# The mLSTM value and output-gate slabs by seven products of halves, as fillers of the attention

## The chip, the cores and the metric

The kernel runs on one core of a Trainium2 chip. The core has a matrix engine (TensorE, PE in the rows), a vector engine (VectorE, DVE), a scalar engine (ScalarE, ACT), GpSimd (POOL), and a sync engine (SP) that here only issues transfers and waits for semaphores. Each engine works through its own list in order; semaphores tie the lists together. The metric is the device time of one execution in microseconds (us). Everything is float32.

## What is computed

One layer of a decoder trunk on 256 tokens of width 2048: a norm, one input projection that feeds three mixers (a sparse attention with a compressed, a selected and a window branch; an mLSTM; a convolution), one output projection, a residual add, a second norm, and a mixture of 32 experts of which each token takes two.

```python
(q, k_c, v_c, k_s, v_s, k_w, v_w, g_nsa, mq, mk, mv, mo, mi, mf, cu) = jnp.split(h @ w_in, points, axis=-1)
a_out = nsa_attention(q, k_c, v_c, k_s, v_s, k_w, v_w, g_nsa, ...)
hm = mlstm_chunkwise(mq, mk, mv, mi + mlstm_i_bias, mf + mlstm_f_bias)
hm = jax.nn.sigmoid(mo) * hm
...
return jnp.concatenate([a_out, hm, c], axis=-1) @ w_out
...
hb = jax.nn.silu(xb @ w_gate[e]) * (xb @ w_up[e])      # for each expert e
y += (hb @ w_down[e]) * wt
```

The change concerns `mv` and `mo`: 1024 columns of `h @ w_in`, four slabs of 256 columns (`mv0`, `mv1`, `mo0`, `mo1`).

## The kernel before

**Slabs and units.** The input weights come in slabs of 2048 x 256 into a ring of six slots in SBUF (`ring`, slab n in slot n mod 6). Fifteen slabs (`FAST_SLABS`) are multiplied by seven products of halves: the 256 tokens, the 2048 inputs and the 256 columns are halved, and seven products of 128 x 1024 by 1024 x 128 (`m1` to `m7`, each 8 matmuls of 128 columns on TensorE) with sums on VectorE take the place of eight. The token sums (`tok_s1` to `tok_s4`) are made once and lie in `x1`. The weight sums are made for each slab by VectorE: `left_sums` (two instructions), `right_sum` and `last_sum` (one each), all on 128 x 1024 elements, and seven short adds put the products together (`combine`, and the copy in `keep_m1`). The last four slabs, `mv0` to `mo1`, are plain: 8 units of 16 matmuls of 256 columns, 128 in all.

**The attention.** Those 128 matmuls are fillers: `fill(n)` puts the next n of them between the steps of the attention, so that TensorE has work while VectorE and ScalarE work on the scores. The attention has four parts s = 0 to 3. `scores(s, n)` multiplies queries by keys, pair by pair (8 pairs in parts 0 and 1, 4 in parts 2 and 3), with n fillers behind each pair; each pair waits until VectorE has taken the pair before it out of the one PSUM buffer (`biased`). On VectorE `biases(s)` adds the position term to each pair and reduces for the maximum after every second pair (every pair in parts 2 and 3). ScalarE takes the exponents, VectorE scales them (`gated(s)`, which ends in `p_ready`), and `attend(s, n)` on TensorE transposes them block by block and multiplies by the values, with n fillers in each block (5 blocks in parts 0 and 1). The order on TensorE is scores 0, scores 1, attend 0, scores 2, attend 1, scores 3, `mlstm_values`, and then attend 2, attend 3 and the output projection; on VectorE it is biases 0, biases 1, gated 0, gated 1, biases 2, and so on. The scores of parts 0 and 2 lie in `spare`, those of parts 1 and 3 in `x1`, whose token sums are done with by then. ScalarE copies each finished plain unit out of PSUM (`late_saves`).

**The output projection and the experts.** The output weights come in four column parts m (`OUT_SLOTS` names the ring slots). Part 0 runs as plain matmuls (`out_part`), parts 1 to 3 by seven products of halves (`product`). SP then streams 403 MB of expert weights through the ring and other buffers; every transfer waits for the TensorE product that frees its buffer (`load_chunk`: `prod_done` in the output projection, `w_used` in the experts).

Of the kernel before, what the change touches and what calls it, by code (L numbers as in the profile page):

```python
# [19 lines left out]
ALU = mybir.AluOpType  # L20
# [3 lines left out]
P = 128  # L24
# [3 lines left out]
DK = D // P  # L28
# [10 lines left out]
RING = 6  # L39
# [149 lines left out]
UNITS = projection_units()  # L189

FAST_SLABS = ("ca0", "ca1", "mq0", "mq1", "mk0", "mk1", "vc0", "ks0", "kw0", "vs0", "q0", "q1", "q2", "q3", "vw0")
FAST = [u for u, (n, _, kind, _, i) in enumerate(UNITS) if SLABS[n] in FAST_SLABS and i == 0]
# [26 lines left out]
LATE = units_before("mv")  # L219


# [17 lines left out]
CHUNK_SLOT = [3, 4, 0, 5, 1, 2]  # L239
CHUNK_INC = 16  # L240
# [52 lines left out]
TILES_BY = [sum(2 * HPG * (t + 1) for p, t in STEPS[:s]) for s in range(len(STEPS) + 1)]  # L293
LATE_STEPS = (len(UNITS) - LATE) * DK
SLOPES = [2.0 ** (-8.0 * (h + 1) / HEADS) for h in range(HEADS)]


def build(nc, x, attn_norm_g, w_in, cmp_pos_k, cmp_w1_k, cmp_w2_k, cmp_pos_v, cmp_w1_v, cmp_w2_v, nsa_out_g,
# [3 lines left out]
    with ExitStack() as ctx:  # L302
# [10 lines left out]
        x1 = sb("x1", [P, TT, D])  # L313
# [20 lines left out]
        def mb(name, shape, dt=F32):  # L334
# [41 lines left out]
        sc = [tile.rearrange("p (g h b k) -> p g h b k", g=2, h=HPG, b=2)  # L376
              for tile in (att[:, :], x1[:, :, :].rearrange("p t d -> p (t d)"))]
        osq = hid[:, :]
# [50 lines left out]
        tok_21, tok_22 = hT[:, 0:8, P:2 * P], hT[:, 8:16, P:2 * P]  # L429
        in_t3, in_t2 = (tile[:, :, :].rearrange("p a b -> p (a b)").rearrange("p (k n) -> p k n", k=8) for tile in (mv, mo))  # L430

        def quarter(u, high, right):
# [215 lines left out]
        def _(sp):  # L648
# [268 lines left out]
        def _(pe):  # L917
# [117 lines left out]
            def mlstm_values():  # L1035
                pe.wait_ge(unit_saved, units_with("mv"))
                pe.wait_ge(biased, TILES_BY[-1])
# [124 lines left out]
            def late_step():  # L1162

                u, k = LATE + late[0] // DK, late[0] % DK
                n, part, kind, s, i = UNITS[u]
                if k == 0:
                    pe.wait_ge(w_loaded[n % RING], slab_at[n])
                    pe.wait_ge(unit_saved, LATE - 2 if u == LATE else u - 1)
                mm = pe.matmul(PS[:, unit_bank(u), 0:256], hT[:, k, i * P:(i + 1) * P], ring[:, n % RING, k, :],  # L1169
                               start=(k == 0), stop=(k == DK - 1))  # L1170
                if k == DK - 1:
                    mm.then_inc(unit_done, 1)
                late[0] += 1
# [686 lines left out]
        def _(act):  # L1860
# [132 lines left out]
            def save_unit(u):  # L1993
# [14 lines left out]
                elif kind == "folded":  # L2008
                    b = b[:, 0:128].rearrange("p (t n) -> p t n", t=TT)
                    step(act.activation(gates[:, :, 0:48], b[:, :, 0:48], ACT.Sigmoid, bias=ZERO_C))  # L2010
                    return act.activation(gates[:, :, 48:56], b[:, :, 48:56], ACT.Copy)
                elif part == "mv":
                    dst = mv[:, i, s * 256:(s + 1) * 256]
                elif part == "mo":
                    dst = mo[:, i, s * 256:(s + 1) * 256]
                elif part in ("kc", "vc"):
# [27 lines left out]

            late = [LATE]

            def late_saves(n):
                for u in range(late[0], late[0] + n):
                    act.wait_ge(unit_done, u + 1)
                    save_unit(u).then_inc(unit_saved, 1)  # L2050
                late[0] += n

            def exponents(s, saves):

                p, t = STEPS[s]
                u, w = s % 2, P * (t + 1)
                for i in range(HPG):
# [6 lines left out]
                    e.then_inc(exp_done, 1)  # L2064
                    if i == 1:
                        late_saves(saves)
                act.wait_ge(cmp_shifted, s + 1)
# [18 lines left out]

            def attend_saves(s, saves):
                for j in range(len(BLOCKS_OF[s])):
                    turned_saves(s, j)
                    if s == 3 and j == 1:  # L2090
                        pieces["mlstm_root"]()
                    if j == 3:
                        late_saves(saves)
                head_saves(s)
# [4 lines left out]

            exponents(0, 0)  # L2100
            late_saves(1)
            exponents(1, 1)
            late_saves(2)
            attend_saves(0, 1)
            exponents(2, 0)
            late_saves(1)
            attend_saves(1, 1)
            head_root(0)
            exponents(3, 0)
            late_saves(1)  # L2110
            act.wait_ge(unit_saved, len(UNITS))
            act.activation(mo[:, :, :], mo[:, :, :], ACT.Sigmoid, bias=ZERO_C).then_inc(mo_gated, 1)
            head_root(1)
            attend_saves(2, 0)
            attend_saves(3, 0)
            mlstm_result()
# [206 lines left out]
        def _(dve):  # L2323
# [364 lines left out]
            def mlstm_norm():  # L2688
# [3 lines left out]
                    .then_inc(hm_norm, 1)  # L2692

            biases(0)
# [456 lines left out]
```

## Time and profile before

| | before |
|---|---|
| median of 3 runs | 1425.89 us (1425.21 to 1428.28) |
| the profiled execution's own time | 1428.03 us |
| its span, first to last instruction | 1426.2 us |
| TensorE busy | 1205.7 us, 85% of the span |
| VectorE busy | 483.6 us, 34% |
| ScalarE busy | 255.3 us, 18% |
| HBM read | 476.05 MB, 335 GB/s over the span |
| chain that ended last | TensorE 52%, transfers 43% |

How to read it: an engine's busy time is the sum of its instructions. The span lies 1.83 us under the execution's own time. The chain that ended last is followed back from the last instruction, at each step to what released it; work off this chain can grow without cost until it gets onto it. A busy share is a mean over stages with different limits, so the rows below go by stage.

### The profile page before, as it was taken

The page shows a single profiled execution, that of the slowest core. Times are in us where ns is not written, and L with a number is a line of the kernel's source. Part 1 is how long each engine was busy: PE and PEld are TensorE (multiplying, and loading weights), DVE is VectorE, ACT ScalarE, POOL GpSimd, SP SyncE. Part 2 cuts the span into 40 slices and gives each one's busy share as a digit, 9 for nine tenths or more (in the row PEclk, how much of TensorE's full clock was granted, in tenths as well). Part 3 has the DMA queues.
Part 4 walks back from the last instruction along what each step waited for, and adds up shares of the span by engine and source line. Part 5 has one row for each costly group of instructions (what it writes and reads, how often), then busy time and mean ns, then how long its engine had stood idle before and what let it go on. Part 6 is the DMA issues. An engine that isn't in the chain of part 4 may idle for free.

```text
span 1426.2 us, 17903 instructions
## 1 busy us (share of the span) xinstructions
PE 1205.7 (85%) x7431; PEld 708.9 (50%) x7431; DVE 483.6 (34%) x1001; ACT 255.3 (18%) x629; POOL 13.5 (1%) x82
## 2 busy tenths in 40 slices
PE   8999999999999998669689958768587695876977
PEld 7999999766568753123244314224142241422422
DVE  5398997663875431121110220111101111011123
ACT  2101111444600122011111101002020010201112
POOL 2000000000010000000000000000000000000000
PEclk9999999999999999889999989989899898998989
DMA  9958677431644899999999999999999999999995
GB/s 318 274 158 194 167 161 236 119 82 38 165 112 166 346 413 426 429 427 427 428 428 428 426 428 427 427 427 429 428 426 427 429 427 425 431 426 426 429 427 237
DMA packets 133362, 479.34 MB, mean 336 GB/s; under 512 B 47804, under 2 KB 105632, under 8 KB 107552
## 3 DMA queue, kind: packets, MB, share of 16 engines
q1 hardware_dynamic: 126816, 477.58, 85.9%
q10 hardware_dynamic: 6464, 0.58, 0.4%
q8 instruction: 61, 1.00, 0.3%
q14 instruction: 21, 0.17, 0.0%
HBM read 476.05 MB, written 2.10 MB: 335 GB/s over the span
## 4 chain that ended last, share of the span: by engine, by line
PE 52%; DMA 43%; ACTq 2%; DVE 1%; ACT 1%; issue 1%; DVEq 0%
DMA ring<-in_expert_w_up_dram 36%; PE PS L1127 13%; PE PS L1447 10%; DMA spare<-in_expert_w_up_dram 6%; PE PS L1269 5%; PE PS L1169 3%; PE PS L1434 3%; PE PS L1246 2%; PE PS L1638 2%; ACTq L1862 2%; PE PS L1425 1%; PE PS L1221 1%; PE PS L1119 1%; PE PS L1648 1%; PE PS L1188 1%; PE PS L1509 1%
## 5 line engine op out<-in xcount | busy, mean ns | idle before, releaser
L1447 PE MATMUL PS<-ring,XG 128*32 128x512 f32 x1296 | 222.2, 734 | 147.9 <-DMA ring<-in_expert_w_up_dram 107.3
L1447 PEld LDWEIGHTS PS<-ring,XG 128*32 128x32 f32 x1296 | 57.6, 131 | 274.9 <-issue 271.8
L3068 DVE TENSOR_TENSOR hTe<-PS,sg 128x128 f32<-128x128 f32 (+1 forms) x31 | 9.9, 320 | 349.3 <-ACT sg L2193 349.1
L2885 DVE TENSOR_TENSOR x<-PS,x 128x1024 f32<-128x1024 f32 x41 | 50.2, 1225 | 209.8 <-PE PS L1526 208.4
L2181 ACT ACTIVATE Hs<-PS 128x512 f32<-128x512 f32 x30 | 17.9, 597 | 463.1 <-PE PS L1447 349.8
L1434 PE MATMUL PS<-ring,XG 128*64 128x512 f32 x192 | 84.6, 594 | 18.0 <-DMA ring<-in_expert_w_up_dram 14.5
L1526 PE MATMUL PS<-Y,SW 128*128 128x512 f32 (+2 forms) x176 | 90.6, 627 | 1.5 <-ACT ro L2289 1.5
L1447 PE MATMUL PS<-spare,XG 128*32 128x512 f32 x208 | 66.0, 793 | 27.8 <-DMA ring<-in_expert_w_up_dram 27.8
L1436 PE MATMUL PS<-ring,XG 128*64 128x512 f32 x192 | 85.0, 595 | 0.0
L1425 PEld LDWEIGHTS PS<-sel,xn 128*128 128x128 f32 x640 | 75.3, 191 | 13.0 <-issue 12.7
L1425 PE MATMUL PS<-sel,xn 128*128 128x128 f32 x640 | 77.6, 280 | 1.4 <-DVE x L2885 1.4
L1127 PE MATMUL PS<-hT,ring 128*128 128x128 f32 x624 | 73.4, 275 | 0.7 <-ACT mix L2031 0.7
L1127 PEld LDWEIGHTS PS<-hT,ring 128*128 128x128 f32 x624 | 71.7, 192 | 1.9 <-issue 1.7
L3079 DVE COPY Y<-PS 32x512 f32<-32x512 f32 x46 | 31.8, 692 | 118.0 <-PE PS L1509 117.6
L1509 PE MATMUL PS<-ring,hTe 128*32 128x512 f32 x608 | 70.5, 596 | 0.0
L2161 ACT ACTIVATE XG<-PS,ffn_gk 128x128 f32<-128x128 f32 (+1 forms) x176 | 54.1, 358 | 65.3 <-PE PS L1425 54.1
L1169 PE MATMUL PS<-ring,hT 128*128 128x256 f32 x256 | 64.3, 392 | 0.0
L1434 PEld LDWEIGHTS PS<-ring,XG 128*64 128x64 f32 x192 | 25.3, 137 | 71.9 <-issue 71.9
L1169 PEld LDWEIGHTS PS<-ring,hT 128*128 128x128 f32 x256 | 45.8, 189 | 19.7 <-issue 14.9
L1526 PEld LDWEIGHTS PS<-Y,SW 128*128 128x128 f32 (+2 forms) x176 | 29.4, 192 | 41.7 <-issue 39.7
L1127 PE MATMUL PS<-x,ring 128*128 128x128 f32 x416 | 48.6, 275 | 0.0
L2466 DVE SCALAR_TENSOR_TENSOR mix<-spare,taps,mix 128x256 f32<-128x256 f32 x120 | 48.4, 481 | 0.0
(494 smaller groups left out, 1577.2 us busy)
## 6 DMA issues: line engine op xcount, KB each, us to landing
ring<-in_expert_w_up_dram SPq DMA_DIRECT2D x53, 2048.0 KB, 23.8
ring<-in_expert_w_gate_dram SPq DMA_DIRECT2D x53, 2048.0 KB, 26.9
ring<-in_expert_w_down_dram SPq DMA_DIRECT2D x51, 2048.0 KB, 27.1
ring<-in_w_in_dram SPq DMA_DIRECT2D x17, 2048.0 KB, 9.5
spare<-in_expert_w_gate_dram SPq DMA_DIRECT2D x9, 2048.0 KB, 26.2
spare<-in_expert_w_up_dram SPq DMA_DIRECT2D x8, 2048.0 KB, 23.9
spare<-in_expert_w_down_dram SPq DMA_DIRECT2D x8, 2048.0 KB, 27.3
ring<-in_w_in_dram SPq DMA_DIRECT2D x16, 512.0 KB, 7.3
```

Of the source, the lines that this page charges most:

```text
L1127: mm = pe.matmul(dst, left[:, k], right[:, k], start=(k == 0), stop=(k == 7))
L1169: mm = pe.matmul(PS[:, unit_bank(u), 0:256], hT[:, k, i * P:(i + 1) * P], ring[:, n % RING, k, :], start=(k == 0), stop=(k == DK - 1))
L1269: mm = pe.matmul(PS[:, 4 + n // 2, 256 * (n % 2):256 * (n % 2) + 256], left[:, k, :], right[:, k, :], start=(k == 0), stop=(k == 7))
L1425: mm = pe.matmul(PS[:, 6 + f % 2, (k % 2) * P:(k % 2) * P + rows_of_group(q)], xn[:, t, k, :], sel[:, t, 0:rows_of_group(q)], start=(t == ...
L1434: gate = pe.matmul(PS[0:width, bank, :], x_, weight_rows(gate_slot, 4 * (c % 2) + j), start=(c == 0 and j == 0), stop=(c == 3 and j == 3))
L1436: up = pe.matmul(PS[64:64 + width, bank, :], x_, weight_rows(up_slot, 4 * (c % 2) + j), start=(c == 0 and j == 0), stop=(c == 3 and j == 3))
L1447: mm = pe.matmul(PS[r:r + 32, 0, :], gathered_rows(q, 4 * c + j)[:, column:column + 32], weight_rows(slots[u], 4 * (c % 2) + j), start=(c ...
L1509: mm = pe.matmul(PS[32 * b:32 * b + 32, 2, :], hTe[:, k, 0:32], w[:, j, 512 * b:512 * b + 512], start=(k == 0), stop=(k == 3))
L1526: mm = pe.matmul(PS[:, 4 + 2 * cols + b, :], SW[0:rows, buf, t * P:(t + 1) * P], Y2[0:rows, buf, (2 * cols + b) * 512:(2 * cols + b + 1) * ...
L2161: ins = act.activation(gathered_rows(q, k)[:, 0:rows], PS[:, 6 + f % 2, P * i:P * i + rows], ACT.Copy, scale=ffn_gk[:, k:k + 1])
L2466: ins = dve.scalar_tensor_tensor(out=cacc[:, c, :], in0=src, scalar=w, in1=cacc[:, c, :], op0=ALU.mult, op1=ALU.add)
L2885: dve.tensor_tensor(y, new, old, ALU.add).then_inc(sc_added, 1)
```

## The change

The four slabs `mv0` to `mo1` join the slabs that are multiplied by seven products of halves. The fillers are now 4 x 7 x 8 = 224 matmuls of 128 columns instead of 128 of 256 columns. VectorE makes the weight sums of each slab (`late_left_sums`, `late_right_sums`, `late_end_sum`: four instructions) and puts the products together (`late_first`, `late_last`: eight short ones), placed by hand between the parts of the attention; ScalarE's copies of the units go. The token sums stay in `x1` until the fillers are done, so that the scores of parts 1 and 3 move from `x1` to ring slot 1, and the weight sums lie in ring slot 2. The output weights and the expert chunks take the ring slots in another turn. The first two column parts of the output weights now go into slots that the last four slabs leave, and wait for those.

```diff
-OUT_SLOTS = [(1, 2), (3, 4), (0, 5), (1, 2)]
+OUT_SLOTS = [(3, 4), (5, 0), (1, 2), (3, 4)]
-TURN = [SPARE, 3, 4, 0, 5, 1, 2]
+TURN = [SPARE, 5, 0, 1, 2, 3, 4]
...
             for m, pair in enumerate(OUT_SLOTS):
-                if m < 3:
+                if m < 2:
                     sp.wait_ge(unit_done, max(last_use[s] for s in pair))
-                else:
-                    sp.wait_ge(p_turned, 2 * PAIRS_BY[-1])
+                elif m == 2:
                     for t in range(TT):
                         sp.dma_start(x1[:, t, :], x[0, t * P:(t + 1) * P, :]).then_inc(x_again, 16)
+                    sp.wait_ge(p_turned, 2 * PAIRS_BY[-1])
+                else:
                     sp.wait_ge(out_done, TT)
...
             def late_step():
+                i, r = divmod(late[0], 8 * len(LATE_PRODUCTS))
+                name, k = LATE_PRODUCTS[r // 8], r % 8
+                j, u = FAST_LATE + i, LATE_SLABS[i]
                 if k == 0:
+                    if name == "m2":
+                        pe.wait_ge(first_scaled if i else unit_saved, SCALED + 2 * i - 1 if i else LATE - 2)
+                    if name == "m5":
+                        pe.wait_ge(first_scaled if i else unit_saved, SCALED + 2 * i if i else LATE)
+                    if name in ("m6", "m4"):
+                        pe.wait_ge(w_summed, 4 * j + {"m6": 3, "m4": 4}[name])
+                mm = pe.matmul(late_part(name), tokens[:, k], weights[:, k], start=(k == 0), stop=(k == 7))
...
-            fill(8)
+            fill(16)
             pe.wait_ge(unit_saved, LATE)
             pe.wait_ge(cmp_saved, 1)
-            scores(0, 2)
+            scores(0, 5)
             scores(1, 3)
-            fill(16)
+            fill(32)
             pe.wait_ge(sT_ready, ML_H)
-            attend(0, 4)
-            scores(2, 3)
-            attend(1, 4)
+            attend(0, 7)
+            scores(2, 5)
+            fill(1)
+            attend(1, 7)
             mean_square(0)
-            scores(3, 3)
+            scores(3, 5)
             fill(LATE_STEPS)
             mlstm_values()
             pe.wait_ge(conv_out, CT)
-            pe.wait_ge(unit_saved, len(UNITS))
+            pe.wait_ge(first_scaled, LATE_SAVED)
...
+            late_left_sums(0)
+            late_right_sums(0)
+            late_end_sum(0)
+            late_left_sums(1)
             biases(0)
+            late_first(0)
+            late_last(0)
+            late_right_sums(1)
             biases(1)
+            late_end_sum(1)
             gated(0)
+            late_first(1)
+            late_left_sums(2)
+            late_last(1)
             gated(1)
+            late_right_sums(2)
+            late_end_sum(2)
+            late_first(2)
             biases(2)
+            late_last(2)
+            late_left_sums(3)
+            late_right_sums(3)
+            late_end_sum(3)
             head_squares(0)
             gated(2)
+            late_first(3)
             biases(3)
+            late_last(3)
             head_norm(0)
```

Among the fillers the products of a slab come in the order m2, m1, m6, m7, m5, m3, m4. Product m2 of a slab waits for `late_first` of the slab before it (its PSUM bank), m6 for the slab's right sum, and m4 for its end sum.

Two places show how the lists of the engines move. The first is VectorE's list behind the last slab of the input projection: the rows of before run from the last add of that slab to the first maximum of the scores of part 0. `spare` holds those scores, `w` the compressed ones.

```order
L2425 TENSOR_TENSOR PS<-PS,pT 128x128
L2618 SCALAR_TENSOR_TENSOR w<-dist_c,PS 128x16
L2620 SCALAR_TENSOR_TENSOR spare<-dist,PS 128x2x128
L2618 SCALAR_TENSOR_TENSOR w<-dist_c,PS 128x16
L2620 SCALAR_TENSOR_TENSOR spare<-dist,PS 128x2x128 x3
L2625 TENSOR_REDUCE rs<-spare 128x2x2
```

The same place in the changed list, from the same last add to the first score row; lines 2709 to 2727 are weight sums.

```order
L2434 TENSOR_TENSOR PS<-PS,pT 128x128
L2709 TENSOR_TENSOR ring<-ring 128x1024
L2712 TENSOR_TENSOR ring<-ring 128x8x128
L2719 TENSOR_TENSOR ring<-ring 128x1024
L2727 TENSOR_TENSOR ring<-ring 128x8x128
L2709 TENSOR_TENSOR ring<-ring 128x1024
L2712 TENSOR_TENSOR ring<-ring 128x8x128
L2627 SCALAR_TENSOR_TENSOR w<-dist_c,PS 128x16
```

Six instructions of 128 x 1024 elements now stand between the input projection and the first scores. The second place is VectorE's list between the scores of part 0 and those of part 1 in the changed kernel; before, the first score row of part 1 followed the row of line 2639 (2630 then) directly. `mv`, `upto` and `cmask` take the put-together products here.

```order
L2639 TENSOR_TENSOR w<-w,rs 128x128
L2735 COPY upto<-PS 128x128
L2736 TENSOR_TENSOR mv<-PS,upto 128x128
L2737 TENSOR_TENSOR upto<-PS,upto 128x128
L2738 TENSOR_TENSOR cmask<-PS,upto 128x128
L2747 TENSOR_TENSOR upto<-PS,upto 128x128
L2748 TENSOR_TENSOR mv<-PS,cmask 128x128
L2749 TENSOR_TENSOR mv<-PS,cmask 128x128
L2751 TENSOR_TENSOR mv<-PS,upto 128x128
L2719 TENSOR_TENSOR ring<-ring 128x1024
L2627 SCALAR_TENSOR_TENSOR w<-dist_c,PS 128x16
```

Nine instructions, eight short and one of 128 x 1024, moved in between two parts of the scores.

## Rows read from the trace of the kernel before

**Rows 1.** The page: its head line and the transfer engines' line of the slices.

```profile
span 1426.2 us, 17903 instructions
...
DMA  9958677431644899999999999999999999999995
```

**Rows 2.** Windows by stage: stretch, length; busy (count) PE, PEld, DVE, ACT, POOL; clock, DMA share, GB/s.

```profile
265.90:308.40 42.50, 41.58 (x194) 27.64 (x193) 29.92 (x86) 24.81 (x81) 0.00 (x0) 1.00 0.40 100
...
478.00:552.00 74.00, 71.78 (x538) 43.98 (x534) 23.22 (x95) 20.71 (x54) 0.00 (x0) 1.00 0.99 408
552.00:1426.20 874.20, 664.45 (x3842) 274.33 (x3842) 129.62 (x212) 118.37 (x278) 0.00 (x0) 0.91 0.99 420
```

**Rows 3.** The chain that ended last, in order of time: start, length, what.

```profile
412.58 37.99 PE PS L1269 x176
...
553.98 15.95 DMA ring<-in_expert_w_up_dram
```

**Rows 4.** SP's waits from 430 to 510: total, times, longest.

```profile
SPq L687 <- PE PS L1269: 62.6, 5, 25.0
```

**Rows 5.** The same chain: a fast slab, and plain fillers in one piece, in twos and threes.

```profile
252.24 12.50 PE PS L1127 x112
...
266.05 3.46 PE PS L1169 x16
...
270.17 1.06 PE PS L1169 x4
...
287.15 1.49 PE PS L1169 x6
```

**Rows 6.** VectorE's timeline, 249 to 329: start, length, line, tiles, [wait and releaser].

```profile
249.04 1.23 DVE L2383 TENSOR_TENSOR mv<-ring 128x1024 f32<-128x1024 f32 x1 [5.14 <-PE PS L1127]
250.30 1.23 DVE L2386 TENSOR_TENSOR ring<-ring 128x1024 f32<-128x1024 f32 x1
...
265.98 0.29 DVE L2425 TENSOR_TENSOR PS<-PS,pT 128x128 f32<-128x128 f32 x1
...
271.93 0.75 DVE L2620 SCALAR_TENSOR_TENSOR spare<-dist,PS 128x256 f32<-128x256 f32 x2 [0.81 <-PE PS L1188]
272.72 1.22 DVE L2625 TENSOR_REDUCE rs<-spare 128x4 f32<-128x1024 f32 x1
...
303.77 4.29 DVE L2649 TENSOR_SCALAR spare<-spare,rs 128x256 f32<-128x256 f32 x16
...
328.21 0.17 DVE L2618 SCALAR_TENSOR_TENSOR w<-dist_c,PS 128x16 f32<-128x16 f32 x1 [14.46 <-PE PS L1188]
```

**Rows 7.** TensorE's timeline, 272 to 309, same columns.

```profile
272.88 0.73 PE L1188 MATMUL PS<-keys,nsa_q 64*128 64x272 f32 x4
...
276.51 0.73 PE L1188 MATMUL PS<-keys,nsa_q 64*128 64x272 f32 x4
...
286.45 0.70 PE L1188 MATMUL PS<-keys,nsa_q 64*128 64x256 f32 x4 [0.45 <-DVE x L2620]
...
308.41 1.06 PE L1203 MATMUL PS<-ident,spare 128*128 128x128 f32 x8
```

**Rows 8.** Window of one load of output weights, columns as in Rows 2.

```profile
308.40:325.90 17.50, 17.49 (x95) 12.19 (x96) 5.21 (x21) 6.17 (x12) 0.00 (x0) 1.00 0.97 240
```

**Rows 9.** TensorE's timeline behind four waits in the expert stage.

```profile
599.74 5.34 PE L1447 MATMUL PS<-ring,XG 128*32 128x512 f32 x32 [4.73 <-DMA ring<-in_expert_w_up_dram]
...
707.43 3.64 PE L1447 MATMUL PS<-ring,XG 128*32 128x512 f32 x32 [2.09 <-DMA ring<-in_expert_w_up_dram]
...
836.28 4.08 PE L1447 MATMUL PS<-ring,XG 128*32 128x512 f32 x24 [3.39 <-DMA ring<-in_expert_w_up_dram]
...
895.05 0.61 PE L1434 MATMUL PS<-ring,XG 128*64 128x512 f32 x1 [2.72 <-DMA spare<-in_expert_w_up_dram]
```

**Rows 10.** Windows right behind the last two of these waits, columns as in Rows 2.

```profile
836.30:840.30 4.00, 4.00 (x28) 1.25 (x32) 0.00 (x0) 0.00 (x0) 0.00 (x0) 0.67 1.00 426
...
895.10:899.10 4.00, 4.00 (x20) 1.69 (x22) 0.00 (x0) 0.00 (x0) 0.00 (x0) 1.00 0.98 418
```

More of the change, by code:

```diff
@@ L219 @@
 LATE = units_before("mv")
+LATE_SLABS = [u for u in FAST if u >= LATE]
+FAST_LATE = len(FAST) - len(LATE_SLABS)
+LATE_PRODUCTS = ["m2", "m1", "m6", "m7", "m5", "m3", "m4"]
+LATE_STEPS = 8 * len(LATE_PRODUCTS) * len(LATE_SLABS)
+SCALED = 2 + FAST_LATE
+LATE_SAVED = SCALED + 2 * len(LATE_SLABS)
 HIDDEN_UNIT = units_before("w1v")
@@ L376, in build @@
         sc = [tile.rearrange("p (g h b k) -> p g h b k", g=2, h=HPG, b=2)
-              for tile in (att[:, :], x1[:, :, :].rearrange("p t d -> p (t d)"))]
+              for tile in (att[:, :], ring[:, 1, :, :].rearrange("p k n -> p (k n)"))]
         osq = hid[:, :]
@@ L430, in build, with late_part @@
         in_t3, in_t2 = (tile[:, :, :].rearrange("p a b -> p (a b)").rearrange("p (k n) -> p k n", k=8) for tile in (mv, mo))
+        late_sums = ring[:, 2, :, :].rearrange("p k n -> p (k n)").rearrange("p (s a k n) -> p s a k n", s=2, a=2, k=8)
+        late_a, late_b = upto[:, :], cmask[:, :]
+        def late_part(name):
+            q = LATE_PRODUCTS.index(name)
+            return PS[:, q // 4, P * (q % 4):P * (q % 4) + P]
         def quarter(u, high, right):
@@ L1162, in late_step @@
             def late_step():
-                u, k = LATE + late[0] // DK, late[0] % DK
-                n, part, kind, s, i = UNITS[u]
+                i, r = divmod(late[0], 8 * len(LATE_PRODUCTS))
+                name, k = LATE_PRODUCTS[r // 8], r % 8
+                j, u = FAST_LATE + i, LATE_SLABS[i]
+                n = UNITS[u][0]
                 if k == 0:
[L1167 to L1171, printed above, removed]
+                    if name == "m2":
+                        pe.wait_ge(w_loaded[n % RING], slab_at[n])
+                    if name == "m2":
+                        pe.wait_ge(first_scaled if i else unit_saved, SCALED + 2 * i - 1 if i else LATE - 2)
[3 more added lines that the diff above has]
+                        pe.wait_ge(w_summed, 4 * j + {"m6": 3, "m4": 4}[name])
+                tokens, weights = {"m1": (tok_11, quarter(u, 0, 0)), "m2": (tok_12, quarter(u, 1, 0)),
+                                   "m3": (tok_s4, quarter(u, 1, 1)), "m4": (tok_22, quarter(u, 1, 0)),
+                                   "m5": (tok_s1, quarter(u, 0, 1)), "m6": (tok_s2, late_sums[:, i % 2, 1]),
+                                   "m7": (tok_s3, late_sums[:, i % 2, 0])}[name]
+                mm = pe.matmul(late_part(name), tokens[:, k], weights[:, k], start=(k == 0), stop=(k == 7))
+                if k == 7 and name in ("m2", "m7"):
+                    mm.then_inc(prod_done, 1)
+                if k == 7 and name in ("m3", "m4"):
                     mm.then_inc(unit_done, 1)
@@ L2042, in _, with exponents @@
                     pieces[name]()
[L2045 to L2053, printed above, removed]
+            def exponents(s):
                 p, t = STEPS[s]
@@ L2692, in mlstm_norm, with late_left_sums @@
                     .then_inc(hm_norm, 1)
+            def late_left_sums(i):
+                j, u = FAST_LATE + i, LATE_SLABS[i]
+                n = UNITS[u][0]
+                dve.wait_ge(w_loaded[n % RING], slab_at[n])
+                dve.wait_ge(unit_done, LATE if i < 2 else LATE_SLABS[i - 2] + 2)
+                dve.tensor_tensor(late_sums[:, i % 2, 0], quarter(u, 1, 1), quarter(u, 0, 1), ALU.subtract)\
+                    .then_inc(w_summed, 1)
+                dve.wait_ge(w_summed, 4 * j + 1)
+                dve.tensor_tensor(quarter(u, 0, 1), quarter(u, 0, 1), quarter(u, 0, 0), ALU.subtract)\
+                    .then_inc(w_summed, 1)
@@ new lines, in late_right_sums, with late_end_sum @@
+            def late_right_sums(i):
+                j, u = FAST_LATE + i, LATE_SLABS[i]
+                dve.wait_ge(w_summed, 4 * j + 2)
+                dve.tensor_tensor(late_sums[:, i % 2, 1], quarter(u, 1, 1), quarter(u, 0, 1), ALU.subtract)\
+                    .then_inc(w_summed, 1)
+            def late_end_sum(i):
+                j, u = FAST_LATE + i, LATE_SLABS[i]
+                dve.wait_ge(prod_done, 2 * j + 1)
+                dve.wait_ge(w_summed, 4 * j + 3)
+                dve.tensor_tensor(quarter(u, 1, 0), quarter(u, 1, 0), late_sums[:, i % 2, 1], ALU.subtract)\
+                    .then_inc(w_summed, 1)
@@ new lines, in late_first @@
+            def late_first(i):
+                _, part, _, s, _ = UNITS[LATE_SLABS[i]]
+                dst, c = mv if part == "mv" else mo, 256 * s
+                dve.wait_ge(prod_done, 2 * (FAST_LATE + i) + 2)
+                step(dve.tensor_copy(late_a, late_part("m1")))
+                issued(dve.tensor_tensor(dst[:, 0, c:c + P], late_part("m2"), late_a, ALU.add))
+                step(dve.tensor_tensor(late_a, late_part("m6"), late_a, ALU.add))
+                dve.tensor_tensor(late_b, late_part("m7"), late_a, ALU.add).then_inc(first_scaled, 1)
@@ new lines, in late_last @@
+            def late_last(i):
+                u = LATE_SLABS[i]
+                _, part, _, s, _ = UNITS[u]
+                dst, c = mv if part == "mv" else mo, 256 * s
+                dve.wait_ge(unit_done, u + 2)
+                dve.wait_ge(first_scaled, SCALED + 2 * i + 1)
+                both = issued(dve.tensor_tensor(late_a, late_part("m5"), late_a, ALU.add))
+                issued(dve.tensor_tensor(dst[:, 1, c:c + P], late_part("m4"), late_b, ALU.add))
+                issued(dve.tensor_tensor(dst[:, 1, c + P:c + 2 * P], late_part("m5"), late_b, ALU.add))
+                dve.wait_ge(dve_step, both)
+                dve.tensor_tensor(dst[:, 0, c + P:c + 2 * P], late_part("m3"), late_a, ALU.add).then_inc(first_scaled, 1)
```

40 lines of the change are left out of this document (14 added, 26 removed).

## The prediction

> **What bounds the kernel now.** I read the page first: transfers are at nine tenths from slice 16 on [rows 1]. The windows by stage say when that begins: from 552 us to the end the transfer engines are busy 0.99 of the time at 420 GB/s, and TensorE idles 210 of 874 us [rows 2]. In the stretch of the change, 265.9 to 308.4 us, it is the other way round: transfers 0.40, TensorE busy 41.6 of 42.5 us, VectorE 29.9 [rows 2]. The chain in order of time agrees: it runs on TensorE through the output projection (412.58 to 450.57 in one piece) and turns to transfers at 553.98 [rows 3]. So two questions follow. Does the attention end earlier or later, and does that shift the stream of expert weights?
>
> The second is quickly answered. SP issues those transfers behind waits for products of the output projection, 62.6 us of waits in five [rows 4]. Transfers are bound to TensorE's progress before they saturate, so a shift of the attention's end shifts the whole stream, one to one. The reader should look at who waits in the attention, then: TensorE waits for VectorE there 0.45 us at most [rows 7], but VectorE is close behind, since a score pair cannot start until the pair before it is out of PSUM.
>
> **The change, step by step.** *TensorE's own work.* A fast slab is 56 matmuls of 128 columns; each leaves two records, and 112 records take 12.50 us: 0.223 us a matmul. The 16 records of eight plain fillers take 3.46 us: 0.4325 us [rows 5]. So the fillers cost 224 x 0.223 = 50.0 us instead of 128 x 0.4325 = 55.4: a gain of 5.4 us. Behind score pairs a group of fillers takes some 0.19 us more than its matmuls (two: 1.06 against 0.865; three: 1.49 against 1.30) [rows 5]; I keep 0.19 for groups of five.
>
> Here a rule speaks against the change. The Trainium skill, page TensorE: Matmul & The Clock Gate, section Back-to-back issue gap, gives 81 ns for a matmul of 128 columns in a stream with its weight load, against some 56 ns alone. By that ratio, as an estimate, the 224 would cost some 72 us and the kernel would lose about 22 us more than in my sum. The trace disagrees: its fast slab has a weight load for every matmul and keeps 0.223 us, half of the wide one's 0.4325 within 4% [rows 5].
>
> *VectorE's new work.* A sum of 128 x 1024 takes 1.23 us, and the next starts 1.26 us later if it waits for it [rows 6]. Sixteen of them are 20 us, and 32 short adds of 0.29 us (next start after some 0.2, 0.3 where one waits for the last) [rows 6] another 8. VectorE has room for this as a mean, for instance 14.46 us in one wait behind the first half of the attention [rows 6]. But the sums stand at fixed places, so I follow both engines in time. Durations used: bias of a score pair 0.75 us (0.85 with its compressed part), maximum 1.22, scaling of a part 5.5 (4.29 for sixteen instructions and six short ones) [rows 6], a score pair 0.66 to 0.7 until the next matmul, 0.73 to its end [rows 7].
>
> 1. *Before the first scores.* VectorE is free at 266.2, when its last add of the projection has started and drained [rows 6]. Six sums come first: 266.2 + 6 x 1.23 = 273.6. The first pair is out of PSUM 0.85 us later, and TensorE's second pair starts at 274.6. TensorE would be there at 271.6 (266.05, 16 x 0.223, a pair 0.7, five fillers 1.3). A wait of 3.0 us.
> 2. *Scores 0.* Two pairs took 3.63 us (272.88 to 276.51) [rows 7], a round trip between the engines. With five fillers TensorE itself needs 2 x (0.66 + 1.31) = 3.94. The eighth pair starts at 274.6 + 3 x 3.94 = 286.4.
> 3. *Between scores 0 and 1.* The ninth pair ends TensorE's useful work at 289.0: the next filler is m2 of slab 1, which needs `late_first` of slab 0. VectorE gets the eighth pair at 287.1, and needs 0.75 + 1.22 + 0.75 (three short ones) + 1.1: 290.9. A wait of 1.9 us. TensorE then runs three fillers and waits again, since `late_last`, a right sum and the bias of the ninth pair (0.9 + 1.23 + 0.85) come next: until 293.9, a wait of 2.1. The tenth pair was at 286.45 [rows 7]: **+7.4 us**.
> 4. *Scores 1.* With three narrow fillers instead of three wide ones TensorE (before: some 4.28 a round, two groups of 1.49 and two pairs) is faster than the round trip of 3.63, which sets the pace. Three rounds: 3 x 0.65 = **-1.95**. The sixteenth pair is at 304.8.
> 5. *Into attend 0.* VectorE: 305.5 + 0.75 + 1.22 + 0.75 + an end sum 1.23 + `gated(0)` 5.5 = 315.0. TensorE has 0.66 + 35 x 0.223 + 0.19 = 8.7 us of work and is there at 313.5. A wait of 1.5. Before, attend 0 started at 308.41 [rows 7]: now **+6.6**.
> 6. *Attend 0.* Five groups of seven fillers (1.56) for four wide ones (1.73): -0.85. But `late_right_sums(2)` stands behind `gated(1)`: 315.0 + 1.1 + 2.4 + 0.85 + 5.5 + 1.2 = 326.0, and TensorE wants m6 of slab 2 at 324.0, in the third block. A wait of 2.0. Now **+7.75**.
> 7. *Scores 2 and 3, attend 1.* Eight groups of 5 x 0.223 for 3 x 0.4325 (-0.18 each), five groups as in step 6, one more group of one (+0.2 beyond its share, and its 0.2): -1.9. VectorE's sums lie in its waits here. Now **+5.85**.
> 8. *Behind scores 3.* `late_last(3)` stands ahead of `head_norm(0)`, on which `mean_square(1)` waits; 0.9 us on VectorE, of which TensorE sees some 0.5. **+6.3 us** at the output projection.
>
> *Costed at nothing.* ScalarE's eight copies go; TensorE waited for none of them. The output weights come later: a load takes 17.5 us [rows 8]. The second part is issued when the last filler is done, at about 371, lands by 389 and is wanted by VectorE near 403, some 14 us of cover; if that went, each us late would cost one. The third is issued at the end of the attention, near 393, and wanted 40 us later. x comes back earlier than before. The new turn of slots keeps the order in which products free them.
>
> *Sum.* The profiled execution took 1428.03 us, 2.1 over the median of the runs; 1428.03 + 6.3 = 1434.3 for it, and 1425.89 + 6.3 = **1432.2 us** as a median. Unknown are the extra 0.19 of a group (0.1 to 0.25 would make the sum 4.7 to 7.4) and the waits' exact sizes, some 0.3 us each at six places: 4 to 8.5 us, 1430 to 1434.5.
>
> **The rivals.** *The clock falls in the new waits.* Behind a wait of 3.39 us the granted clock was at 0.67 in the mean of the next 4.0 us, so at the lower of its two levels (1.2 GHz instead of 2.4) for most of it; behind one of 2.72 it stayed at full [rows 9, 10]. The first new wait, 3.0 us, lies between. The price: 32 records took 5.34 us behind a wait of 4.73, and 3.64 behind one of 2.09 [rows 9], 1.7 us, and twice that if it lasts. With +6.3 that is 1434 to 1435.6 us. The Trainium skill, page TensorE: Matmul & The Clock Gate, section HAM oscillation — how this bites in real kernels, says that waits for data between bursts of matmuls put the matrix engine back to half clock; the trace agrees for the longer waits, and for 3.0 us no row decides.
>
> *The weight sums hide, and the kernel is faster.* The place is VectorE's list between 266 and 315 us, where the sums add 6 x 1.23 + 2.0 + 1.23 + 1.23 = 11.9 us. If VectorE's waits there (0.81 us before each second pair [rows 6], and its idle time before the first pair) took up all but 5 us of them and step 6 did not wait, the gain of 5.4 us would win. It decides at a sum of new waits of 5.2 us; at half of that the time would be 1423. Against it: the six sums stand ahead of the first score in one piece, and the round trip of the scores leaves no place in between.
>
> *Nothing to see.* Waits of 5 us instead of the 11 that I count: 1425 to 1428. For it: fillers of 128 columns may follow score pairs without the 0.19, which takes some 2.5 us off. *A late load of output weights* would add up to 5 us, 1437; its cover of 14 us speaks against it.
>
> **How the numbers follow.** A measurement of this kernel tells 0.2%, 2.85 us, from no change. My forecast has 0.63 (slower, 1430 to 1434.5), the clock 0.12, the late load 0.04, nothing to see 0.13, hidden sums 0.08. So slower 0.79, same 0.13, faster 0.08. The range reaches from the upper edge of nothing to see, 1428, to 1436.5, past the clock's case.
>
> **What would show it.** Right: in the changed profile the fillers at 0.22 us; TensorE waiting for VectorE some 3 us at the second score pair, about 2 us twice at the tenth, 1.5 us at attend 0 and 2 us inside it; the output projection starting near 418.7 instead of 412.6, and expert transfers saturated as before. Wrong: scores 0 starting without a wait, fillers above 0.25 us, a clock under 1.00 between 270 and 300 us, or an end that doesn't move with the output projection.

## The result, and the profile after

The changed kernel takes 1437.17 us (median of six runs, 1436.19 to 1439.91) beside 1426.75 of before: a ratio of 1.0074 [1.0062, 1.0085], 10.6 us slower (8.8 to 12.1). The direction was forecast and the place too; the size was not, since 1437.17 lies above the range, whose end was 1436.5. The forecast, 1432.2, is missed by 5.0 us. Of these, 0.9 is the median of before itself (1425.89 when the forecast was made); the other 4 are the subject here.

Of after, the profiled execution took 1436.19 us (before 1428.03). The page: head line, busy times, granted clock and transfers over 40 slices.

```profile
span 1434.4 us, 18335 instructions
...
PE 1224.1 (85%) x7623; PEld 718.7 (50%) x7623; DVE 509.9 (36%) x1049; ACT 253.1 (18%) x621; POOL 13.6 (1%) x82
...
PEclk9999999999999999779999988969879798887999
DMA  9958677013576699999999999999999999999996
```

Transfers are at nine tenths from the same slice on as in [rows 1], the fifteenth of 40 (the prediction says 16). The chain in order of time says when, and SP's waits from 430 to 520 say that the transfers are bound as before:

```profile
422.42 37.99 PE PS L1297 x176
...
563.83 16.18 DMA ring<-in_expert_w_up_dram
```

```profile
SPq L701 <- PE PS L1297: 62.1, 5, 25.0
```

The long piece of the output projection starts 9.84 us later than in [rows 3] and the first stretch of expert transfers in the chain 9.85 later; SP waits 62.1 us in five, beside 62.6 in [rows 4]. So nothing was added or given back between the two, and the loss is made before 422 us. Behind 564 us these two executions differ the other way, by some 1.6 us (their spans lie 8.2 apart); that is less than the 3.1 us between the executions of before. TensorE's timeline ahead of 422 us has all the waits of the forecast and one thing more.

```profile
266.22 3.74 PE L1196 MATMUL PS<-ring,hT 128*128 128x128 f32 x32
...
274.84 0.70 PE L1216 MATMUL PS<-keys,nsa_q 64*128 64x256 f32 x4 [2.92 <-DVE spare L2629]
...
291.27 0.91 PE L1196 MATMUL PS<-ring,hT 128*128 128x128 f32 x6 [2.01 <-DVE cmask L2738]
...
294.12 1.22 PE L1216 MATMUL PS<-keys,nsa_q 64*128 64x256 f32 x4 [1.95 <-DVE ring L2629]
295.27 1.65 PE L1196 MATMUL PS<-ring,hT 128*128 128x128 f32 x6
...
307.42 0.70 PE L1216 MATMUL PS<-keys,nsa_q 64*128 64x256 f32 x4 [0.48 <-DVE ring L2629]
...
317.92 1.06 PE L1231 MATMUL PS<-ident,spare 128*128 128x128 f32 x8 [1.78 <-DVE w L2660]
...
328.68 1.38 PE L1196 MATMUL PS<-ring,x 128*128 128x128 f32 x10 [1.75 <-DVE ring L2719]
```

Five new waits: 2.92, 2.01, 1.95, 1.78 and 1.75 us, all for VectorE. The thing more is in the lengths behind the third: a score pair takes 1.22 us instead of 0.70, six records of fillers 1.65 instead of the 0.94 that they take elsewhere. Windows over this place (busy times as in [rows 2], the seventh figure is the granted clock) show why: it fell from 1.00 to 0.50, the lower level, 1.2 GHz.

```profile
286.00:290.00 4.00, 3.26 (x24) 2.26 (x23) 2.87 (x8) 2.16 (x10) 0.00 (x0) 1.00 0.00 0
290.00:294.00 4.00, 0.91 (x6) 0.74 (x6) 3.83 (x14) 1.74 (x7) 0.00 (x0) 0.99 0.00 0
294.00:298.00 4.00, 3.88 (x14) 2.36 (x14) 2.04 (x4) 0.57 (x3) 0.00 (x0) 0.50 0.02 4
298.00:302.00 4.00, 4.00 (x20) 2.89 (x20) 1.97 (x7) 1.50 (x7) 0.00 (x0) 0.66 0.00 0
302.00:306.00 4.00, 3.52 (x24) 2.10 (x22) 3.16 (x8) 2.08 (x8) 0.00 (x0) 1.00 0.00 0
```

In the window before the fall TensorE worked 0.91 of 4 us. VectorE's timeline names the work that it waited for: six weight sums ahead of the first score row (line 2627), then the put-together (line 2738 releases the second wait) and a right sum (line 2719) between the scores of parts 0 and 1.

```profile
266.50 1.21 DVE L2709 TENSOR_TENSOR ring<-ring 128x1024 f32<-128x1024 f32 x1
...
272.74 1.23 DVE L2712 TENSOR_TENSOR ring<-ring 128x1024 f32<-128x1024 f32 x1
273.88 0.16 DVE L2627 SCALAR_TENSOR_TENSOR w<-dist_c,PS 128x16 f32<-128x16 f32 x1
...
290.83 0.29 DVE L2738 TENSOR_TENSOR cmask<-PS,upto 128x128 f32<-128x128 f32 x1
...
292.03 1.22 DVE L2719 TENSOR_TENSOR ring<-ring 128x1024 f32<-128x1024 f32 x1
```

### The profile page after: what moved, and what is told of

It is laid out like the page before. It is cut to its first block, busy times and chain, and to the rows that moved or that the text cites. A ratio compares the mean times of both kernels' runs of the same rounds, so it can differ in the third digit from the quotient of the medians.

```text
span 1434.4 us, 18335 instructions
## 1 busy us (share of the span) xinstructions
PE 1224.1 (85%) x7623; PEld 718.7 (50%) x7623; DVE 509.9 (36%) x1049; ACT 253.1 (18%) x621; POOL 13.6 (1%) x82
## 4 chain that ended last, share of the span: by engine, by line
PE 51%; DMA 41%; DVE 4%; ACTq 2%; issue 1%; ACT 1%; DVEq 0%; SPq 0%
DMA ring<-in_expert_w_up_dram 33%; PE PS L1142 13%; PE PS L1476 10%; DMA spare<-in_expert_w_up_dram 6%; PE PS L1297 5%; PE PS L1463 4%; PE PS L1196 2%; PE PS L1667 2%; DMA ring<-in_expert_w_gate_dram 2%; PE PS L1274 2%; ACTq L1891 2%; PE PS L1454 1%; PE PS L1216 1%; PE PS L1249 1%; PE PS L1134 1%
## 5 line engine op out<-in xcount | busy, mean ns | idle before, releaser
L1476 PE MATMUL PS<-ring,XG 128*32 128x512 f32 x1296 | 233.2, 763 | 132.5 <-DMA ring<-in_expert_w_up_dram 94.9
L1463 PE MATMUL PS<-ring,XG 128*64 128x512 f32 x192 | 92.7, 639 | 14.7 <-DMA ring<-in_expert_w_up_dram 11.9
L1465 PE MATMUL PS<-ring,XG 128*64 128x512 f32 x192 | 94.6, 650 | 0.0
L1476 PE MATMUL PS<-spare,XG 128*32 128x512 f32 x208 | 70.9, 845 | 25.3 <-DMA ring<-in_expert_w_up_dram 25.3
L1142 PEld LDWEIGHTS PS<-x,ring 128*128 128x128 f32 x416 | 47.5, 192 | 0.0
L2220 ACT ACTIVATE Y<-PS 32x512 f32<-32x512 f32 x46 | 27.0, 586 | 89.4 <-PE PS L1538 89.1
```

The source lines that it names most:

```text
L1142: mm = pe.matmul(dst, left[:, k], right[:, k], start=(k == 0), stop=(k == 7))
L1463: gate = pe.matmul(PS[0:width, bank, :], x_, weight_rows(gate_slot, 4 * (c % 2) + j), start=(c == 0 and j == 0), stop=(c == 3 and j == 3))
L1465: up = pe.matmul(PS[64:64 + width, bank, :], x_, weight_rows(up_slot, 4 * (c % 2) + j), start=(c == 0 and j == 0), stop=(c == 3 and j == 3))
L1476: mm = pe.matmul(PS[r:r + 32, 0, :], gathered_rows(q, 4 * c + j)[:, column:column + 32], weight_rows(slots[u], 4 * (c % 2) + j), start=(c ...
```

## The experiments

The theory after the result: VectorE's new instructions stand where TensorE waits for what is behind them; the waits cost more than the 5.4 us that the narrow fillers give, and they lower TensorE's clock besides. Its rivals: the narrow fillers are dearer than their matmuls; the new turn of ring slots with its later loads; the clock falls for another reason. Times over before are worked out from the ratio and the median of before that was measured beside it. Where the start of the output projection is compared, it is the start of its seven-product part, in before:

```profile
412.41 7.07 PE L1269 MATMUL PS<-ring,mix 128*128 128x256 f32 x32
```

**Only the layout.** Before with the changed `OUT_SLOTS`, `CHUNK_SLOT`, `TURN`, issue order of the output weights and place of the scores of parts 1 and 3; plain fillers.

```diff
-              for tile in (att[:, :], x1[:, :, :].rearrange("p t d -> p (t d)"))]
+              for tile in (att[:, :], ring[:, 1, :, :].rearrange("p k n -> p (k n)"))]
```

> The kernel before with the changed turn of ring slots, the later issue of the output weights and the scores of parts 1 and 3 in ring slot 1 instead of x1; the fillers stay plain. My theory (the loss comes from VectorE's new instructions, for which TensorE waits some 11 us against a gain of 5.4, and from a clock fall of 2.4 us behind two of these waits) expects no change from before: within 1.5 us, the output projection starting within 0.5 us of 412.4. The rival that the later output weights or the moved scores cost the time expects 5 to 10 us over before, with a wait for a transfer in the output projection or slower score steps.

1425.99 us, ratio 1.0005 [0.9996, 1.0013]: at most 1.9 us over before. The output projection starts where it did, 0.17 us from the 412.41 of before. The layout is not it.

```profile
412.58 7.07 PE L1270 MATMUL PS<-ring,mix 128*128 128x256 f32 x32
```

**Without the weight sums.** Each of the 16 sums becomes a bare semaphore increment, so the products use halves that are not summed.

```diff
-                dve.tensor_tensor(late_sums[:, i % 2, 1], quarter(u, 1, 1), quarter(u, 0, 1), ALU.subtract)\
-                    .then_inc(w_summed, 1)
+                dve.sem_inc(w_summed, 1)
```

> The changed kernel without the 16 weight sums of the last four slabs (the products take the halves unsummed; the 32 short instructions that put the products together stay). My theory expects the 3 us wait at the second score pair, the 1.75 us wait inside attend 0 and most of the second wait between the parts of the scores to be gone, one wait of about 1.9 us at the ninth pair to stay, no stretch at half clock, and 1 to 3 us less than before (8.5 to 10 less... that is 11 to 13 us less than the changed kernel). The rival that fillers of 128 columns cost more between score steps than their matmuls expects it to stay 3 to 8 us above before.

1428.23 us, ratio 1.001 [1.0, 1.0019]: 0 to 2.7 us over before, neither the gain of my theory nor the 3 to 8 of its rival. Of TensorE's long waits one is left, and less than half of the next:

```profile
287.97 0.91 PE L1196 MATMUL PS<-ring,hT 128*128 128x128 f32 x6 [2.01 <-DVE cmask L2730]
289.69 1.22 PE L1216 MATMUL PS<-keys,nsa_q 64*128 64x256 f32 x4 [0.82 <-DVE ring L2629]
...
303.00 0.70 PE L1216 MATMUL PS<-keys,nsa_q 64*128 64x256 f32 x4 [0.48 <-DVE ring L2629]
...
312.12 1.07 PE L1231 MATMUL PS<-ident,spare 128*128 128x128 f32 x8 [0.41 <-DVE w L2660]
```

Most of the loss goes with the sums, as the theory says. But the pair at 289.69 takes 1.22 us: 2.01 and 0.82 us of waiting with 0.9 of work between them lowered the clock too, against my expectation. From there to the sixteenth pair it takes 13.31 us, where a kernel at full clock below takes 10.90 (293.84 to 304.74). By that, an estimate, the fall cost 2.4 us; without it the output projection, at 414.29, would be 0.5 ahead of before, less than the 1 to 3 that I expected.

**TensorE kept busy in two waits.** Useless matmuls into a bank of PSUM (the memory that TensorE writes its products to) that is free there, behind the ninth pair and ahead of the tenth.

```diff
+                        if pairs[0] == 9:
+                            busy_work(7)
...
+                        if pairs[0] == 9:
+                            pe.wait_ge(sT_ready, ML_H)
+                            busy_work(7)
```

> The changed kernel with seven useless matmuls of 128 columns into a free PSUM bank in each of the two 2 us waits between the scores of part 0 and part 1 (behind the ninth pair, and ahead of the tenth). If these two waits lower the clock, it now stays at 1.00 from 285 to 310 us, the sixteenth score pair starts near 305 instead of 307.4, and the time is 2.4 us under the changed kernel's, 7.5 to 8 over before. If the clock falls for another reason, the stretch at half clock stays and the time is that of the changed kernel, about 10 over before.

1435.63 us, ratio 1.0064 [1.0045, 1.0083], 6.4 to 11.8 over before, the runs from 1431.97 to 1439.5. The clock is at 1.00 from 282 to 310 us, and yet the sixteenth pair is at 308.36:

```profile
275.50 1.23 PE L1222 MATMUL PS<-keys,nsa_q 64*128 64x256 f32 x4 [2.91 <-DVE spare L2638]
276.66 2.50 PE L1196 MATMUL PS<-ring,x 128*128 128x128 f32 x10
...
297.47 0.70 PE L1222 MATMUL PS<-keys,nsa_q 64*128 64x256 f32 x4 [0.38 <-DVE ring L2638]
```

In this execution the clock fell behind the first wait, the one that had left it at full before: ten records take 2.50 us instead of 1.38. The expectation had no place for that. Of the 3.6 us from 304.74, where the pair stands at full clock below, 1.0 is an input projection that ended later in this execution (266.89 instead of 265.93). So the clock held where the waits were filled and fell behind one that was open; which of the open ones it falls behind is not fixed.

**Two slabs.** Only `mo0` and `mo1` by seven products; `mv0` and `mv1` are plain, and the sums stand where VectorE waited.

```diff
-              "mv0", "mv1", "mo0", "mo1")
+              "mo0", "mo1")
...
+            biases(0)
+            biases(1)
+            gated(0)
             late_left_sums(0)
             late_right_sums(0)
+            gated(1)
```

> Only the two output-gate slabs mo0 and mo1 by seven products, mv0 and mv1 plain (64 wide fillers first, then 112 narrow ones); the weight sums stand in places where VectorE waited. My theory expects 2.7 us less work on TensorE, some 0.4 us of group extras, no new wait over 0.5 us before attend 0, some 0.7 us before the mean square of part 1, and so 1 to 2 us less than before. The rival that narrow fillers cost more than their matmuls expects 1 to 4 us more than before.

1424.66 us, ratio 0.999 [0.9981, 0.9998]: 0.3 to 2.7 us under before, as expected. No wait before attend 0 is over 0.45 us, the one before the mean square of part 1 is 0.88, and the output projection starts at 411.00, 1.4 ahead of before, where price, extras and that wait were expected to give 1.6 (2.7 less 0.4 and 0.7). Narrow fillers cost what their matmuls say.

**All three score waits filled.** As two experiments above, and twelve useless matmuls behind the first pair.

```diff
+                        if pairs[0] in (1, 9):
+                            if pairs[0] == 1:
+                                pe.wait_ge(sT_ready, ML_H)
+                            busy_work(12 if pairs[0] == 1 else 7)
```

> The changed kernel with useless matmuls of 128 columns in all three new waits around the scores of part 0: twelve behind the first score pair, seven behind the ninth, seven ahead of the tenth. If the fall of the clock in one or the other of these waits is what the time has beyond the waits themselves, the clock is now at 1.00 from 262 to 326 us, the output projection starts 2 to 3 us earlier than in the changed kernel (419.3 to 420.3), and the time is 6.5 to 7.5 us over before, with less spread than 1432 to 1439.5. If something else is behind it, the time stays 9 to 10.5 over before.

1433.27 us, ratio 1.0052 [1.0038, 1.0065]: 5.4 to 9.3 over before, the runs from 1431.72 to 1434.21. The clock is 1.00 from 262 to 326. The output projection is at 421.22 in the profiled execution, later than expected, since now the clock fell behind the wait inside attend 0:

```profile
262.00:326.00 64.00, 58.15 (x441) 47.50 (x440) 52.71 (x138) 27.28 (x84) 0.00 (x0) 1.00 0.19 46
```

```profile
326.00 2.42 PE L1196 MATMUL PS<-ring,x 128*128 128x128 f32 x10 [1.76 <-DVE ring L2730]
```

**One sum moved.**

```diff
+            late_right_sums(2)
             gated(1)
-            late_right_sums(2)
```

> The changed kernel with one instruction of VectorE moved: the right sum of slab 2 ahead of the scaling of part 1 (gated(1)) instead of behind it. My theory expects the 1.75 us wait inside attend 0 to go and nothing to come in its place: the output projection starts 1.5 to 1.9 us earlier (near 420.5), and the time is 8 to 9 over before. The rival that VectorE is late in any case, so that the wait turns up at the first block of attend 1, expects no change from the changed kernel.

1434.94 us, ratio 1.0064 [1.005, 1.0077]: 7.1 to 11.0 over before, beside 8 to 9 expected and 8.8 to 12.1 of the changed kernel, so the total can't tell. The stage can:

```profile
274.91 1.22 PE L1216 MATMUL PS<-keys,nsa_q 64*128 64x256 f32 x4 [2.92 <-DVE spare L2629]
...
293.99 1.28 PE L1196 MATMUL PS<-ring,hT 128*128 128x128 f32 x6 [2.01 <-DVE cmask L2738]
296.85 1.23 PE L1216 MATMUL PS<-keys,nsa_q 64*128 64x256 f32 x4 [1.57 <-DVE ring L2629]
...
310.27 0.70 PE L1216 MATMUL PS<-keys,nsa_q 64*128 64x256 f32 x4 [0.48 <-DVE ring L2629]
...
320.76 1.06 PE L1231 MATMUL PS<-ident,spare 128*128 128x128 f32 x8 [1.78 <-DVE w L2660]
...
349.94 1.14 PE L1231 MATMUL PS<-ident,ring 128*128 128x128 f32 x8 [0.22 <-ACT mix L2094]
```

From the start of attend 0 to that of attend 1's second block it is 29.18 us. The changed kernel has this row at 349.12 and needs 31.20:

```profile
349.12 1.14 PE L1231 MATMUL PS<-ident,ring 128*128 128x128 f32 x8 [0.22 <-ACT mix L2094]
```

The wait is gone and nothing came in its place, also at attend 1. But in this execution the clock fell twice ahead of attend 0, so that attend 0 starts 2.84 later than in the changed kernel's and the output projection, expected near 420.5, at 423.07. The second fall came behind the wait of 2.01 us alone: the six records behind it take 1.28 us instead of 0.91, ahead of the next wait.

**The changed kernel once more.**

> The changed kernel once more, beside the other three: 9.5 to 11 us over before, and again a stretch at half clock of some 7 us behind one of the three new waits, whichever it is.

1435.62 us, ratio 1.0079 [1.0065, 1.0092], 9.3 to 13.1 over before. Instead of the one fall expected the clock fell behind three waits, each time for less long; the rows behind the first, third and fourth:

```profile
275.28 2.50 PE L1196 MATMUL PS<-ring,x 128*128 128x128 f32 x10
...
296.47 1.65 PE L1196 MATMUL PS<-ring,hT 128*128 128x128 f32 x6
...
319.15 2.85 PE L1196 MATMUL PS<-ring,hT 128*128 128x128 f32 x14
```

The last cost nothing: TensorE is at the place of the fifth wait 2 us later and hardly waits there. Attend 0 takes 31.21 us, as in the first execution.

**The same work at other places.** Slab 0's left and right sums go into VectorE's wait in the last projection slab, a sum or half of a put-together goes between the two pairs of a score round, and the right sum of slab 2 moves as above.

```diff
-            finish(14)
...
+            keep_m1(14)
             late_left_sums(0)
             late_right_sums(0)
+            combine(14)
+            late_left_sums(1)
             late_end_sum(0)
-            late_left_sums(1)
-            biases(0)
-            late_first(0)
-            late_last(0)
-            late_right_sums(1)
-            biases(1)
-            late_end_sum(1)
+            biases(0, {0: lambda: late_right_sums(1), 2: lambda: late_first(0)})
+            biases(1, {0: lambda: late_last(0), 2: lambda: late_end_sum(1)})
```

> All four slabs by seven products, with VectorE's instructions at other places: the left and right sums of slab 0 go into VectorE's 5 us wait in the last slab of the projection (their buffer in ring slot 1), the right and end sums and the put-togethers of slabs 0 and 1 go between the two pairs of a score round, where VectorE waited 0.8 to 1.0 us, and the right sum of slab 2 ahead of the scaling of part 1. The same work on both engines. My theory, that the place of these instructions makes the loss, expects no wait over 0.7 us before attend 0 is over, the clock at 1.00 there, and 1 to 3 us less than before. The rival that VectorE has no room for this work wherever it stands expects waits in the score rounds that add up to 5 us, and 1 to 4 us more than before.

1424.77 us, ratio 0.9989 [0.998, 0.9998]: 0.3 to 2.9 under before. With the same 16 sums, 32 short instructions and 224 narrow fillers, 10.6 us slower (11.3 in the changed kernel's run beside this one) became 1.6 faster. TensorE's longest wait before the end of attend 0 is 0.82 us, a little over the 0.7 expected, and the clock is 1.00:

```profile
287.64 0.70 PE L1225 MATMUL PS<-keys,nsa_q 64*128 64x256 f32 x4 [0.82 <-DVE ring L2637]
...
307.91 1.06 PE L1240 MATMUL PS<-ident,spare 128*128 128x128 f32 x8 [0.41 <-DVE w L2670]
```

**The waits with no effect on the clock.** All three score waits filled, seven useless matmuls ahead of attend 0 as well, and the right sum moved.

> Useless matmuls in the three new waits around the scores of part 0 and also in the wait ahead of attend 0 (seven more), and the right sum of slab 2 ahead of the scaling of part 1, so that TensorE stands idle for less than 0.8 us anywhere between 262 and 350 us. What is left is the waits' length without any effect on the clock: clock 1.00 over that stretch, attend 0 at 315.2, attend 1 at 344.4 (29.2 us later), the output projection at 417.5, 5.1 us behind that of before, and a time 4.5 to 5.5 over before. If the clock had nothing to do with the waits, a stretch at half clock is still there and the time is that of the kernel with the moved right sum, 8 to 9 over before.

1432.37 us, ratio 1.0043 [1.003, 1.0056], 4.3 to 8.0 over before with 6.1 as the middle, beside 4.5 to 5.5 expected. Every expected row is met to 0.1 us; the tenth and the sixteenth pair are the second and third row:

```profile
274.56 0.70 PE L1224 MATMUL PS<-keys,nsa_q 64*128 64x256 f32 x4 [0.24 <-DVE spare L2641]
...
293.84 0.70 PE L1224 MATMUL PS<-keys,nsa_q 64*128 64x256 f32 x4 [0.39 <-DVE ring L2641]
...
304.74 0.70 PE L1224 MATMUL PS<-keys,nsa_q 64*128 64x256 f32 x4 [0.48 <-DVE ring L2641]
...
315.15 1.09 PE L1242 MATMUL PS<-ident,spare 128*128 128x128 f32 x8
...
344.42 1.14 PE L1242 MATMUL PS<-ident,ring 128*128 128x128 f32 x8 [0.22 <-ACT mix L2106]
...
417.56 7.07 PE L1308 MATMUL PS<-ring,mix 128*128 128x256 f32 x32
```

The clock over the stretch, in one window:

```profile
262.00:350.00 88.00, 85.29 (x639) 67.86 (x638) 69.05 (x179) 40.05 (x128) 0.00 (x0) 1.00 0.20 49
```

Without the long waits the clock holds. From 262 to 348 us it fell, in one place or more, in each of the six profiled executions in which a new wait of 1.75 us or more was left open, and in none of the six others, whose longest wait up to the end of attend 0 is 0.82 us.

**The moved sums, and the first scores earlier.** The kernel of the same work at other places, and besides:

```diff
-            fill(16)
+            fill(8)
...
-            scores(1, 3)
+            scores(1, 4)
```

> The kernel with the moved sums, with eight fillers fewer ahead of the first scores (8 instead of 16) and one more behind each pair of part 1 (4 instead of 3); the end sum of slab 0 and the put-togethers move one place further back with them. The scores of part 0 start 1.8 us earlier, and since VectorE's round trips set the pace from there to attend 0, my theory expects attend 0 near 306.3 instead of 307.9, and 2.5 to 4 us less than before. The rival that the rounds are full with the sums in them expects waits over 1 us in them and no more than 1.5 us less than before.

1423.12 us, ratio 0.9976 [0.9967, 0.9986]: 2.0 to 4.7 us under before, the fastest of all. Attend 0 starts at 306.63 (306.3 expected), and the output projection 3.5 us ahead of before:

```profile
306.63 1.07 PE L1240 MATMUL PS<-ident,spare 128*128 128x128 f32 x8 [0.43 <-DVE w L2670]
...
408.95 7.07 PE L1306 MATMUL PS<-ring,mix 128*128 128x256 f32 x32
```

## Why the prediction was too low

**What held.** The price of the fillers: 32 records in 3.74 us are 16 matmuls of 0.223 and 0.17 until the last one's end, and the kernel with two slabs gained at the output projection what that price says, to 0.2 us. The waits: forecast 3.0, 1.9, 2.1, 1.5 and 2.0 us, measured 2.92, 2.01, 1.95, 1.78 and 1.75. The places: tenth pair forecast at 293.9, found at 294.12. Step 7 gave 1.84 us, forecast 1.9. A shift of the attention's end goes through to the experts one to one (9.84 at the output projection, 9.85 there), and in all eleven runs the change of the median is within 1.7 us of the shift of the output projection in the profiled execution (5.15 and 6.1 in the kernel with harmless waits, -3.46 and -3.4 in the fastest). The layout's cost, at most 1.9 us, is not told from nothing.

**What failed** is the step that kept the clock out of the sum. The sum had nothing for it; the rival had it at a chance of 0.12 and at one wait only, the 3.0 us before the second pair ("The first new wait, 3.0 us, lies between"). The four other waits were given no chance of a fall; the row of the expert stage that keeps its clock behind 2.72 us [rows 9] was taken as a bound. The runs showed falls behind shorter waits. The six executions with open waits have 18 new ones of 1.75 to 2.92 us, and 9 falls of the clock, at least one in each execution. It fell behind the waits of 2.92 (2.91) in three of four. Between the parts of the scores, where waits of 2.01 and 0.82 to 1.95 us stand with 0.9 us of matmuls between them, it fell in all four executions in which they were open, in one of them ahead of the second wait. It fell behind 1.78 in one of five, and behind 1.75 (1.76) in one of three. With five such places, a fall somewhere was the likeliest case, not one in eight.

**The sizes.** Step 4 had the sixteenth pair at 304.8; it stands at 307.42 in the changed kernel and at 304.74 where no wait touches the clock. From the tenth pair to the sixteenth it is 13.30 us in the one and 10.90 in the other, so the clock's price is 2.4 us, inside the 1.7 to 3.4 that the rival had. One fall cost between 1.2 and 2.7 us elsewhere, and nothing in one place where TensorE would have waited next anyway. The new waits less the gain of the fillers, without the clock, come to 7.2 us: 5.15 at the output projection of the kernel with all waits harmless (417.56 against 412.41), and 2.02 for the wait inside attend 0 that it lacks (31.20 less 29.18). The forecast's sum was 6.3, low by 0.9 over eight steps. That is not in the waits, 10.4 us beside 10.5 forecast, but in what stands between them: the groups of step 6 gave 0.3 to 0.5 us instead of 0.85, and step 8 cost 0.77 instead of 0.5. 7.2 and 2.4 are 9.6 of the 9.85; 0.3 is the later end of the input projection in this execution. The upper end of the range added one fall to the middle of the sum; with the dearer fall, 3.4 us, on top of the sum's own upper bound of 8.5 it would have reached 1437.8 and held the result.

The rule of the Trainium skill, page TensorE: Matmul & The Clock Gate, section HAM oscillation — how this bites in real kernels, that waits between bursts of matmuls put the engine back to half clock, was thus the one to price into the forecast; the runs agree with it, with the clock at 0.50 behind waits of 1.75 to 2.92 us. The other rule cited, of the Trainium skill, same page, section Back-to-back issue gap, does not show here: 0.22 us a matmul stood in every kernel at full clock.

**What stays open.** Which of several waits lowers the clock in a given execution was not controlled: the clock of the same kernel fell behind the third wait once, and behind the first, third and fourth another time. Why a wait lowers it in one execution and not in the next, no run here shows. So the 9 us of the kernel with one sum moved say nothing about the sum; only its stage does.

## What to carry to other kernels

Work that an idle engine takes over is paid at the place where it stands in that engine's list: the same instructions cost 10.6 us in front of what TensorE waited for, and gained 1.6 in gaps that the engine's own timeline showed (5 us in the slab before, 1 us in each score round). When a change adds several waits of about 2 us to TensorE, give each of them a chance of lowering the clock, not the longest alone, and put the price into the sum: here a fall somewhere was the rule. Where the whole time varies by such a fall, judge one moved instruction by its stage in the trace.

## What was not expected of the hardware

Useless work made the changed kernel faster: 26 matmuls that nobody reads, put into three waits, took it from 1434.66 to 1438.65 us (five runs) down to 1431.72 to 1434.21 (five runs beside them). And waits of 2.01 and 0.82 us with 0.9 us of work between them were enough to halve the clock, and so were, in one execution each, 2.01, 1.78 and 1.76 us alone, while one of 2.92 left it at 1.00 in one execution and halved it in three others (2.91 in one of them).
